# Products of the identity at the ends of the dense stages and at the head of the output projection of a two-layer hybrid decoder step

## The reference

```python
def layer(x, l, ...):
    h = rms_norm(x, g_ffn1_pre[l])
    x = x + 0.5 * rms_norm(swiglu(h, w_ffn1_in[l], w_ffn1_out[l]), g_ffn1_post[l])
    mix = mix_layer(rms_norm(x, g_mix_pre[l]), ..., w_in[l], ..., w_out[l])
    x = x + rms_norm(mix, g_mix_post[l])
    h = rms_norm(x, g_ffn2_pre[l])
    x = x + 0.5 * rms_norm(swiglu(h, w_ffn2_in[l], w_ffn2_out[l]), g_ffn2_post[l])
    return x, ...
```

## Time and profile before

| | |
|---|---|
| runs | 2501.26, 2505.3, 2509.03 us, median 2505.3 |
| profiled execution | 2508.6 us, its span 2506.9 us |
| mean granted TensorE clock | 0.959 |
| TensorE busy | 2340.8 us, 93% |
| VectorE, ScalarE, GpSimd busy | 1192.0, 930.7, 144.3 us |

### The profile page before, as it was taken

The page is one execution under the profiler, slowest core; times in us unless marked ns, Lnnn a source line. Parts: engine busy times, 40 slices in busy tenths (PEclk is TensorE's granted clock), DMA queues, the critical chain, the costliest instruction groups (busy, mean ns, idle before and its releaser), DMA issues. The chain is left out here.

```text
span 2506.9 us, 44904 instructions
## 1 busy us (share of the span) xinstructions
PE 2340.8 (93%) x17622; PEld 2084.8 (83%) x17622; DVE 1192.0 (48%) x2080; ACT 930.7 (37%) x1671; POOL 144.3 (6%) x195
## 2 busy tenths in 40 slices
PE   7999999989888799999899999999898887999997
PEld 7999998756556599999899999977565566999997
DVE  6343273254575565342463434622646565643425
ACT  6223242223325554222352323321333265542333
POOL 0000010011222000000000000100213210000000
PEclk8999999989998899999999999999898898999998
DMA  5233333145765543233333333420658545333233
GB/s 140 68 85 84 101 111 124 51 134 175 208 174 172 146 144 86 67 94 85 91 86 83 84 84 102 146 86 21 193 163 238 166 133 179 98 85 84 76 103 95
DMA packets 384957, 290.97 MB, mean 116 GB/s; under 512 B 51808, under 2 KB 368392, under 8 KB 384272
## 3 DMA queue, kind: packets, MB, share of 16 engines
q1 hardware_dynamic: 368128, 234.08, 33.4%
q0 software_dynamic: 16128, 54.54, 7.1%
q10 hardware_dynamic: 528, 0.02, 0.0%
HBM read 274.99 MB, written 13.58 MB: 115 GB/s over the span
## 5 line engine op out<-in xcount | busy, mean ns | idle before, releaser
L218 PE MATMUL ps<-h_hi,w_hi 128*128 128x288 f32 x2400 | 718.2, 299 | 24.1 <-PEq L174 16.8
L219 PE MATMUL ps<-h_lo,w_hi 128*128 128x288 f32 x2400 | 710.0, 296 | 0.0
L220 PE MATMUL ps<-h_hi,w_lo 128*128 128x288 f32 x2400 | 709.8, 296 | 0.0
L242 DVE TENSOR_TENSOR w_lo<-w_raw,w_hi 128x2048 fp32r<-128x2048 f32 x145 | 332.4, 2292 | 341.0 <-ACT w_hi L236 340.9
L218 PEld LDWEIGHTS ps<-h_hi,w_hi 128*128 128x128 f32 x2400 | 452.2, 188 | 30.4 <-issue 24.7
L219 PEld LDWEIGHTS ps<-h_lo,w_hi 128*128 128x128 f32 x2400 | 452.2, 188 | 1.0
L220 PEld LDWEIGHTS ps<-h_hi,w_lo 128*128 128x128 f32 x2400 | 452.0, 188 | 0.0
L236 ACT ACTIVATE w_hi<-w_raw 128x2048 fp32r<-128x2048 f32 x145 | 276.7, 1908 | 163.6 <-PE ps L220 159.3
L218 PE MATMUL ps<-f_a_hi,w_hi 128*128 128x288 f32 x1024 | 302.7, 296 | 0.0
L220 PE MATMUL ps<-f_a_hi,w_lo 128*128 128x288 f32 x1024 | 301.6, 295 | 0.0
L219 PE MATMUL ps<-f_a_lo,w_hi 128*128 128x288 f32 x1024 | 301.5, 294 | 0.0
(11 more groups left out here) (345 smaller groups left out, 3170.9 us busy)
## 6 DMA issues: line engine op xcount, KB each, us to landing
w_raw<-in_w_ffn_in SPq DMA_DIRECT2D x132, 512.0 KB, 5.2
w_raw<-in_w_ffn_out SPq DMA_DIRECT2D x80, 512.0 KB, 5.0
sa_vn<-in_cache_sb_v SPq DMA_DIRECT2D x256, 128.0 KB
w_raw<-in_w_in SPq DMA_DIRECT2D x52, 512.0 KB, 4.4
sa_vn<-in_cache_win_v SPq DMA_DIRECT2D x96, 128.0 KB
w_raw<-in_w_out SPq DMA_DIRECT2D x24, 512.0 KB, 6.7
sa_kn_early<-in_cache_win_k POOLq DMA_DIRECT2D x72, 128.0 KB
sa_vn<-in_cache_win_v SPq DMA_DIRECT2D x16, 512.0 KB
```

The source lines that it names most:

```text
L218: pe.matmul(out, stat_hi, mov_hi, start=start, stop=False, skip_group_check=True)
L219: pe.matmul(out, stat_hi, mov_lo, start=False, stop=False, skip_group_check=True)
L220: return pe.matmul(out, stat_lo, mov_hi, start=False, stop=stop, skip_group_check=True)
L242: dve.tensor_tensor(E["w_lo"][:, slot], E["w_raw"][:, slot], E["w_hi"][:, slot].bitcast(F32), ALU.subtract).then_inc(S["w_lo"], 1)
```

## The change

A helper issues `n` plain products of the identity with itself into one bank, each with `start` and `stop` and with no semaphore. `post_tensor`, which ends the stages "f1", "ou" and "f2" of each layer, calls it with 16 into bank 5, after the product whose end raises `y_done` for the last time. The output projection calls it with 20, as the first thing that TensorE does in that stage, ahead of the wait for the weights. Nothing reads what these products write.

```diff
@@ -210,6 +210,7 @@
 Y_SUM, X_SUM = 6, 7
 LAST_BANK = X_SUM
+SPARE_BANK = 5
 BEHIND_FFN, BEHIND_MIX = 7, 6
@@ -516,6 +517,12 @@
+def keep_busy(pe, E, bank, n):
+
+    for _ in range(n):
+        pe.matmul(E["ps"][:, bank, 0:P], E["ident"][:], E["ident"][:], start=True, stop=True, skip_group_check=True)
@@ -558,6 +565,7 @@
             if q == first + 1 and k == 3:
                 y_sum(pe, E, St, 0, y_adds(units, first + 1))
         mm.then_inc(S["y_done"], 1)
+    keep_busy(pe, E, SPARE_BANK, 16)
@@ -2862,6 +2870,7 @@
                 if q in (0, KC):
                     pe.wait_ge(S["mix_lo"], KC * half + k + 1)
 
+            keep_busy(pe, E, SPARE_BANK, 20)
             post_tensor(pe, E, S, St, hi, lo, KC, 0, 0, operand)
```

## The result

Over 22 runs each the changed kernel takes 2511.76 us (2506.39 to 2519.59) and the kernel before 2505.11 (2496.63 to 2509.74); the ratio is **1.0029**, 95% interval 1.002 to 1.0038. (A ratio here is estimated over all runs of both kernels and is not the quotient of the two medians, which differ by 6.65 us.) The change makes the kernel 5 to 9.5 us slower, 7.2 in the middle. The profiled execution of the changed kernel took 2511.38 us, its span 2509.7.

A forecast was written before the change was run, and what follows sets the result against it. TensorE, busy 93% of the span, was taken to bound the kernel. +9.2 at the ends, less 0.96, 1.91, 0.4, 0.5 and 0.4 returned, gave +5.0 us on the median 2505.3: 2510.3, range 2503 to 2518.

The forecast's parts named there:

- TensorE becomes last at the barrier: Six stage ends: the 16 products end after VectorE, 1.72 us later at four ends and 1.17 at two.
- The sum of 9.2: Six stage ends: total forecast cost of the later barriers, 4 x 1.72 + 2 x 1.17 us, at 0.105 a pass.
- The return at the openings: Openings of the projection and "f2" in layer 0: held clock gives back 0.96 and 1.91 us; layer 1 gives nothing.
- the twin stage: Same stage in the other layer, run without the low clock; the length difference gave the low clock's price, 0.96 and 1.91.
- the h_lo chain: "f2": VectorE's chain behind h_lo sets the pace at full clock; argued from one TensorE wait of 0.43 us.
- the missing 1.0: "f2" of layer 0: low stretch worth 2.9 us in products, price only 1.91; the gap was put down to h_lo.
- "f1" of layer 1 and the ending: "f1" after the loop's jump, expected low again, gives back 0.4 us; the ending's transposes and sum of squares 0.5.
- The head of the output projection: Its 20 products: warm starts and 2 us late starts cancel, 0.2 us gained in each layer, 0.4 in all.
- Products of the identity don't count for the clock: Rival behind every barrier: identity products neither hold nor raise the clock, so +17 us, 2522; chance 0.12.
- A pass takes half as long: Rival at ends and head: products cost nothing at the ends and fit the head's wait, -8 us, 2497; chance 0.06.
- The mixers move: Rival in the mixers: shifted events make their clock losses fall either way by 7 us, 2503 or 2517; chance 0.17.

## Why the prediction was right

**TensorE becomes last at the barrier: shown.** This step carried the sign. The timeline has the idle times exchanged, doubling the count moves every end by the passes added, and a count that stops short of VectorE's end costs nothing (0.1 at one of the four ends without the jump). The sum of 9.2 was 10.5: a pass takes 0.111 us and not 0.105. The pair at L1646 gave the operand shape but only one distance, rounded twice; the eight transposes of the same rows had 0.11. That is 1.1 us over 6 x 32 passes, and 0.2 came with the jump of the loop, which varies by more than that.

**The return at the openings: shown, and of the size read from the twin stage.** Forecast 0.96 and 1.91, in the profile 0.92 and 1.94. The forecast was read from the same profile of before that it is compared with here, so what the new profile adds is that layer 0 now runs at the pace of layer 1; that the fall in "f2" was a dear one in that profile is chance. In the seven profiles whose ends have 14 passes or more, all openings of pr take 187.1 us and all of "f2" 309.0; in the three with fewer (the kernel before among them), pr of layer 0 takes 188.0 and "f2" between 309.04 and 310.95. That layer 1 gives nothing held for pr every time; "f2" of layer 1 was free of the loss only in the profile of before (309.82 and 309.85 in the two others). What the low clock costs in "f2" is therefore more often 0.8 than 1.9 a layer: 1.9 where products ran low for 5.9 us, 0.8 in the four cases where they did for 3.4. That the h_lo chain caps the return was argued from one wait. The profiles bear it out in part: each of the 15 executions of "f2" that opened at full clock has one wait for h_lo of 0.42 to 0.44 us, some 20 us in, and none of the five that ran low has it. That is 0.43 of the missing 1.0; the remainder stays open, and no run took that chain away.

**"f1" of layer 1 and the ending: mis-sized.** I had taken 0.4 and 0.5 back; the profile has +0.2 and, for the ending, +0.7. "f1" stayed at the low clock. In the ending the second eight transposes got faster (1.37 us in place of 1.91), but the last 24 ran low where they had run mostly high before (5.38 us in place of 4.15), after a pause of 7.67 us that the change doesn't touch (7.68 before). Why the clock came out lower there stays open.

**The head of the output projection: right as a balance.** Forecast -0.4 for both layers, measured -0.2 in the changed kernel. The rise was put at 5.0 us behind the barrier for both layers and came at 5.6 and 3.2, so layer 0 lost 0.4 and layer 1 won 0.6; that these nearly cancel is luck. It was also read correctly why: the late start eats the warm start. What I did not draw from it is that 11 products would give the one without the other, 2.6 us in two layers.

**The total.** +5.0 was forecast; the profile without the mixers has +8.7 and the runs +7.2 (5 to 9.5). The 3.7 between +5.0 and +8.7 are 1.3 of passes and jump, 1.8 of "f1" and the ending, 0.2 at the head, and 0.4 of the start, which is no part of the change. The measured 2511.8 lies inside the range. It is just on the near side of the 0.3% that I had named as the edge of "no difference"; but the interval, 0.20% to 0.38%, leaves out zero, so over 22 runs the loss is a real one.

**The rivals.** "Products of the identity don't count for the clock" is refuted by the openings and by the head: after some 26 passes in layer 0 and 15 in layer 1 the clock rises, and nothing but identity had run behind the barrier. "A pass takes half as long" is refuted by 3.73 us for 32; with transposes, which are half as many passes, its consequence at the ends came nearly true (0.1 us at each end of "f1"). "The mixers move" is what the single profiles show: 341.5 to 355.8 us in twenty executions of the same instructions. Over 22 runs it averages out, and no setting of the ends or the head moved it in a way that I could tell.

## What to carry to other kernels

Filler on an engine is free only up to the moment at which another engine arrives at the same barrier or wait: read that slack as a number (here 1.94 us after the last product, 4.74 at the head) and divide it by the measured pass, at the clock that the passes will really have. A filler sized by the pause that one wants to bridge is a new critical path; here 16 cost 7 us, and 7 of the same (9 behind the output projection) gave all of the return at the openings.

## What was not expected

- Among longer pauses, the length does not tell whether the clock falls: 1.93 us was followed by a fall and 3.52 us was not. Shorter ones were safe: at the four openings of pr and "f2" none of the 28 behind a pause of at most 1.78 us fell, and 8 of the 12 behind 1.93 to 3.52 us did (ten profiles). Falls came up to 1.4 us after products had started again (the run with 3 at the ends: "f2" of layer 1 starts at 2161.51, the slice from 2162 has 0.96 and the next 0.50). Yet pr behaved alike from kernel to kernel: pr of layer 0 fell in all three profiles without enough filler, pr of layer 1 in none. Why stays open.
- In the one profile that has them, transposes of the identity keep the clock up just as products do, with half the passes (0.11 us for one 128 x 128 transpose of 32-bit data, 0.22 for a product).
- The jump back of the layer loop and the barrier before it take 6.92 to 7.72 us from the last product in the kernels whose ends are hidden, a spread of 0.8 us, as much as a low opening of "f2" cost in four cases of five.
